# Attention by blocks, groups C and D: ScalarE copies the queries under the shift rows, GpSimd makes their low parts

## The reference

```python
def attend(q, k, v, bias, mask, sink=None):
    s = jnp.einsum('bqhgd,bkhd->bhgqk', qg, k).astype(F32) * (d ** -0.5)
    s = s.reshape(b, hq, tq, -1) + bias
    s = jnp.where(mask, s, NEG_INF)
    ...  # softmax over the keys (and the sink, in C), then the values

def dsa_attend(q, qi, wi, qpos, k, v, ki, kpos, topk, t5_d):
    ...  # sel: the topk keys of each query by the indexer's score
    s = jnp.einsum('bqhd,bqjd->bhqj', q, ks).astype(F32) * (q.shape[-1] ** -0.5) + bias
    s = jnp.where(valid[:, None], s, NEG_INF)
    p = jax.nn.softmax(s, axis=-1).astype(vs.dtype)
    o = jnp.einsum('bhqj,bqjd->bqhd', p, vs)
```

## Time and profile before

| | before |
|---|---|
| median of 3 runs | 4170.81 us (4169.08 to 4173.33) |
| the profiled execution | 4172.25 us, span 4170.4 us |
| mean granted TensorE clock | 0.955 |
| TensorE matmuls (PE) busy | 3779.2 us, 91% of the span |
| TensorE weight loads (PEld) busy | 2628.8 us, 63% |
| VectorE (DVE) busy | 2094.3 us, 50% |
| ScalarE (ACT) busy | 1609.7 us, 39% |
| GpSimd (POOL) busy | 689.1 us, 17% |

### The profile page before, as it was taken

One profiled execution on the slowest core, in us unless ns is written; L12 is line 12 of the kernel. 1 busy time (PEld: TensorE's weight loads), 2 busy tenths in 40 slices (PEclk: granted clock), 3 DMA queues, 4 the chain that ended last, 5 costly groups with the idle time before them and its releaser, 6 DMA issues. The chain is left out here.

```text
span 4170.4 us, 51477 instructions
## 1 busy us (share of the span) xinstructions
PE 3779.2 (91%) x18129; PEld 2628.8 (63%) x18129; DVE 2094.3 (50%) x4989; ACT 1609.7 (39%) x2441; POOL 689.1 (17%) x408
## 2 busy tenths in 40 slices
PE   4899999996999999997999788999868599999798
PEld 3689988995776666665874544444345355555476
DVE  3211111117887344343320199999868766665432
ACT  5111000113454444433320189996445243333332
POOL 4100000002222111111430000000032542211143
PEclk9999999997999999998999899999979699999899
DMA  5222212215455333213431211111242311100243
GB/s 182 66 74 79 67 65 77 68 57 116 98 117 112 72 68 75 65 32 109 163 123 66 63 29 61 61 42 55 97 110 77 89 47 25 37 11 3 107 161 126
DMA packets 222512, 328.50 MB, mean 79 GB/s; under 512 B 22225, under 2 KB 129033, under 8 KB 220897
## 3 DMA queue, kind: packets, MB, share of 16 engines
q1 hardware_dynamic: 173280, 236.21, 19.8%
q10 hardware_dynamic: 43776, 72.50, 4.7%
q0 software_dynamic: 5216, 16.70, 1.9%
HBM read 214.35 MB, written 110.99 MB: 78 GB/s over the span
## 5 line engine op out<-in xcount | busy, mean ns | idle before, releaser
L1028 PE MATMUL attAB_p_o<-attAB_pt,attAB_v 128*65 128x512 f32 (+3 forms) x1120 | 432.8, 484 | 0.2 <-ACT attAB_pt L1075 0.2
L1115 DVE TENSOR_REDUCE attAB_mx<-attAB_p_s 128x1 f32<-128x512 f32 (+2 forms) x360 | 209.5, 609 | 305.7 <-PE attAB_p_s L963 195.0
L508 DVE COPY ab_stage<-ab_pA 128x256 f32<-128x256 f32 (+1 forms) x108 | 56.5, 523 | 602.9 <-PE ab_pA L477 572.3
L2394 DVE TENSOR_SCALAR_CACHE_REDUCE cd_junk<-score,cd_thr 128x512 bf16<-128x512 f32 (+8 forms) x288 | 350.4, 1275 | 1.3 <-DVE cd_thr L2411 0.2
L2432 ACT ACTIVATE cd_gate<-score,cd_thr 128x384 bf16<-128x384 f32 (+2 forms) x192 | 322.3, 1679 | 23.8 <-DVE cd_thr L2411 16.6
L506 ACT ACTIVATE ab_stage<-ab_pA 128x256 f32<-128x256 f32 (+1 forms) x108 | 50.0, 463 | 699.8 <-PE ab_pA L477 679.5
L475 PE MATMUL ab_pA<-ab_W_hi,h_hi 128*128 128x256 f32 x1088 | 309.1, 284 | 3.2 <-PE ab_pA L477 3.1
L1005 PE MATMUL attAB_p_t<-attAB_q_a,attAB_k_a 128*128 128x512 f32 (+3 forms) x560 | 300.2, 540 | 12.7 <-DVE attAB_s_t L1160 11.3
L476 PE MATMUL ab_pA<-ab_W_lo,h_hi 128*128 128x256 f32 x1088 | 307.9, 283 | 0.0
L477 PE MATMUL ab_pA<-ab_W_hi,h_lo 128*128 128x256 f32 x1088 | 307.9, 283 | 0.0
L1637 PE MATMUL attD_p_o<-attD_pt,attD_v 128*65 128x512 f32 x548 | 282.6, 597 | 0.0
(11 more groups left out here) (352 smaller groups left out, 8556.0 us busy)
## 6 DMA issues: line engine op xcount, KB each, us to landing
attAB_raw<-t_k SPq DMA_DIRECT2D x32, 640.0 KB, 7.3
attAB_raw<-t_q SPq DMA_DIRECT2D x32, 640.0 KB, 9.6
t_qg<-cd_stage SPq DMA_DIRECT2D x74, 256.0 KB, 2.0
ab_W_raw<-in_w_ab SPq DMA_DIRECT2D x17, 1024.0 KB, 5.8
mix_o<-t_o SPq DMA_DIRECT2D x34, 512.0 KB, 4.3
t_q<-ab_stage ACTq DMA_DIRECT2D x40, 256.0 KB, 2.0
t_k<-ab_stage ACTq DMA_DIRECT2D x40, 256.0 KB, 2.0
norm_x<-in_x ACTq DMA_DIRECT2D x17, 512.0 KB, 3.7
```

The lines of the kernel that those rows point to most:

```text
L1028: done = nc.tensor.matmul(p_o[u % 2][0:VW, i0 * P:(i0 + n) * P], left, pt[c % NPT][:, at * P:(at + n) * P], start=(c == plan.chunks_of[u][ ...
L2394: nc.vector.tensor_scalar(junk[nth % 2][:, 0:widths[n]], sc[n][:], T[:, n:n + 1], None, ALU.is_ge, ALU.add, accum_out=cnt[s % 2][:, n:n + ...
```

## The change

Four edits, in both stages:

- ScalarE rounds the queries without a factor (L1691, now L1700), and directly behind it makes `q_b` itself, from `q_raw`, with `only_q` as a factor by partition (new, L1701); this counts `q_copied`.
- GpSimd's `prepare` no longer writes `q_b`. In its place it makes the low part in `q_a`, rows 64 to 127, as a subtraction of 64x1024 (L1488), and counts `q_split`. Before it, it waits for its own last instructions of the other kinds, and after it for its own count.
- VectorE's `split_queries` is gone, in the opening and in the loop, and `split_at` with it.
- The factor 1/8 goes into `project_cd`: the evacuations of the query units carry it (L2596), the others a factor of 1.0.

SP's reload of a raw buffer and TensorE's first fill of a block now wait for `q_copied` as well as for `q_split`. The lines behind the edits move: in the changed kernel L1706 is L1716, L1713 is L1723, L1723 is L1733, L1729 is L1739, L1764 is L1774, L1800 is L1804, L1490 is L1496 and L1501 is L1507.

```diff
@@ query_loads
             if b >= NRAW:
                 sp.wait_ge(q_split, b - NRAW + 1)
+                sp.wait_ge(q_copied, b - NRAW + 1)
@@ gpsimd
+                own = {}
+
                 def prepare(b):
                     s = b % NQ
                     pool.wait_ge(q_rounded, b + 1)
-                    nc.gpsimd.tensor_scalar(q_b[s][:], q_a[s][0:AUX].bitcast(F32), only_q[:, 0:1], None, ALU.mult
-                                            ).then_inc(q_copied, 1)
+                    if kind == "D" and b:
+                        pool.wait_ge(near_q, b)
+                    for last, n in own.items():
+                        pool.wait_ge(last, n)
+                    nc.gpsimd.tensor_tensor(q_a[s][HD:P], q_raw[b % NRAW][HD:P], q_a[s][HD:P].bitcast(F32), ALU.subtract
+                                            ).then_inc(q_split, 1)
+                    pool.wait_ge(q_split, b + 1)
@@ add_near and subtract_sinks
                     done.then_inc(near_k, 1)
+                    own[near_k] = b + 1
...
+                    own[sink_less] = u + 1
@@ fill
                         pe.wait_ge(q_split, b + 1)
+                        pe.wait_ge(q_copied, b + 1)
@@ round_queries
-                    nc.scalar.activation(q_a[b % NQ][:], q_raw[b % NRAW][:], ACT.Copy, scale=HD ** -0.5).then_inc(q_rounded, 1)
+                    nc.scalar.activation(q_a[b % NQ][:], q_raw[b % NRAW][:], ACT.Copy).then_inc(q_rounded, 1)
+                    nc.scalar.activation(q_b[b % NQ][:], q_raw[b % NRAW][0:AUX], ACT.Copy, scale=only_q[:, 0:1]).then_inc(q_copied, 1)
@@ vector
-                def split_queries(b):
-                    s = b % NQ
-                    dve.wait_ge(q_copied, b + 1)
-                    nc.vector.scalar_tensor_tensor(q_a[s][HD:P], q_raw[b % NRAW][HD:P], HD ** -0.5, q_a[s][HD:P].bitcast(F32),
-                                                   ALU.mult, ALU.subtract).then_inc(q_split, 1)
...
-                for b in plan.early_blocks:
-                    split_queries(b)
...
-                    for b in plan.split_at[c]:
-                        split_queries(b)
@@ project_cd
-                    nc.scalar.activation(stage[u % 2][:, 0:w], pA[u % BANKS][:, 0:w], ACT.Copy).then_inc(ev[u % BANKS], 1)
+                    scale = HD ** -0.5 if u < 2 * TUNITS else 1.0
+                    nc.scalar.activation(stage[u % 2][:, 0:w], pA[u % BANKS][:, 0:w], ACT.Copy, scale=scale
+                                         ).then_inc(ev[u % BANKS], 1)
```

More of the change, by code:

```diff
@@ L1272, in __init__ @@
         self.blocks_at = [[] for _ in range(NT)]
-        self.split_at = [[] for _ in range(NT)]
         self.near_at = [[] for _ in range(NT)]
@@ L1300, in __init__ @@
                     self.blocks_at[ready].append(p)
-                    self.split_at[max(min(ready + 2, first_fill[u] - 1), ready)].append(p)
                     self.near_at[due[u]].append(p)
```

## The result

The changed kernel takes 4150.70 us, the median of 5 runs (4148.13 to 4152.39); before it was 4170.81. The ratio is 0.995, with a 95% interval of 0.9936 to 0.9965: 20.1 us less. The profiled execution has a span of 4150.6 us, against 4170.4. The forecast was 4157.5, the range 4145 to 4173.

A forecast was written before the change was run, and what follows sets the result against it. The prediction took VectorE to set C's loop, with TensorE 0.72 us a block behind, and TensorE to set D's. C +3.65 and D -16.9 gave -13.3: 4172.25 to 4158.95, median 1.44 lower, 4157.5 us; range 4145 to 4173.

The forecast's parts named there:

- The projection: Projection ahead of C and D: evacuations get an immediate factor instead of 1; taken as zero, 4.3 us of ScalarE at worst.
- C's opening: Start of C: block 2's query path shorter, -1.8; TensorE's wait of 1.25 goes but ScalarE's extra pass stands there, -0.2.
- C's loop: 26 units of C: VectorE's removed pass gives -6.95, ScalarE's new pass costs 1.05 in 12 blocks, +12.6; sum +5.65.
- D's first wait: D's opening, TensorE's 10.97 wait for the first shift: VectorE splits cached keys from 3264.0 to 3266.3, ending earlier, -4.6.
- rival A: D's opening: port changes hands at each GpSimd boundary, cached-key split ends at 3262.1, another 4.2 us gained, 4153.3; chance 0.12.
- The second wait: D's opening, TensorE's 9.36 wait for block 2's queries: fills come at 3285.05 instead of 3291.99, -6.95.
- The third wait: D's opening, fourth block: shift is ready before TensorE comes, -3.56; the clock's fall behind the wait goes too, -1.8.
- D's loop: Loop of D: VectorE's 1.2 us and ScalarE's extra 1.05 a block are hidden beside TensorE, 0.
- Rival C: Loop of D: ScalarE's pass makes TensorE wait, 1.15 in each of the last 15 blocks, +17.3, 4174.8; chance 0.14.
- Rival B: Loop of C: ScalarE's pass costs nothing because TensorE has slack that busy time hides, -12.6, 4144.9; chance 0.10.
- rival D: D's opening: GpSimd's work stays one queue, cached-key split comes last, TensorE's 3.56 wait stays; D gives 9.4, 4165.0; chance 0.14.

The follow-up runs named there:

- the kernel with it and the form alone: Kernel before, with factor 1/8 in the projection and VectorE's low-part pass as plain subtraction; GpSimd still writes q_b: 4170.72 us, ratio 1.0001.
- the gap: Changed kernel with ScalarE's q_b pass two chunks later for blocks 4 and up, between an exponent and the next shift rows: 4137.83 us, ratio 0.9917.
- the keep: Changed kernel with ScalarE's q_b pass one chunk later for blocks 4 and up, behind `keep` and ahead of the unit's second exponent: 4144.20 us.
- the doubled pass: Changed kernel with ScalarE's 66x1024 pass done twice a block, the second into a spare tile, in both stages: 4190.27 us, one run.
- GpSimd keeps both: Changed kernel with the pass over q_b back on GpSimd, ahead of its subtraction: 4173.10 us.
- GpSimd keeps its pass, VectorE doesn't wait for it: Kernel before with factor in projection and plain VectorE subtraction, GpSimd's q_b pass reading raw queries, VectorE waiting for ScalarE's copy alone: 4159.70 us.

## Why the prediction was right, and where it was not

The sign, the places and which of them gains or loses were right; the size was 13.3 where the median moved by 20.1, and 4150.7 lies below the forecast's own range of 4152 to 4164. By its steps:

- **The projection**, zero: 576 and 577 ns, and the kernel with it and the form alone has a ratio of 1.0001.
- **C's opening**, -1.8 and -0.2. The first fill of block 2 came at 3073.16 against 3075.70, 2.54 earlier, of which 0.77 are keys and a start that came earlier (the shift rows ahead of it at 3066.67 against 3067.44): 1.77 for 1.8. Behind it another 1.78 went (-4.32 in all at the second turn), where the prediction had let ScalarE's first pass take up nearly all of it. That pass fell into the first unit of the loop instead.
- **C's loop**, -6.95 + 12.6 = +5.65: measured +6.93. Thirteen passes lie in the 26 units, not twelve; 13 x 1.05 = 13.65, and -6.95 + 13.65 = +6.7. The unit lengths of 4.18 and 5.2 came as written (4.17 and 5.25). Together with the opening and the end, C cost 2.03 where the forecast had 3.65. That the pass is paid because of its place was only argued then; the gap, the keep and the doubled pass show it.
- **D's first wait**, -4.6. This is the step that failed. The split of the cached keys got in at the end of the near tile, as rival A had it at a chance of 0.12, and ended at 3264.20. The first shift rows came at 3265.62 for 3272.35, and C had ended 2.03 later: 8.76 gained in C's frame, where rival A's price was 8.8. The two first waits together gave 15.70 for 4.6 + 6.95 = 11.55. The prediction took the pattern from VectorE's passes of before, with the same near tiles in GpSimd's queue; but ahead of those near tiles stood GpSimd's pass over q_b, which the change takes away. That the earlier entry comes from this is not shown (last section).
- **The second wait**, -6.95. The fill of block 2 came 13.69 earlier, 15.72 in C's frame, and the first shift rows, ahead of it, 8.76 (above): 6.96 is left for this one.
- **The third wait**, -3.56 - 1.8 = -5.36: measured 5.38, between the turns around it. The clock's share is not separated from the wait's.
- **D's loop**, 0: 0.6 us remain there, less than runs differ. Rival C (ScalarE's pass stalls D) fell with the doubled pass: 1.8 us of D's stage for twice the work.
- **Rival B** (the pass costs nothing in C) fell with the waits of 0.91 for the exponent, **rival D** (GpSimd bounds D's opening) with the first wait at 3.92 and the third gone.

With -8.8 in place of -4.6 the working gives -17.5; the 1.6 in C and the 0.6 of D's loop make it -19.7, against 19.65 at D's last turn.

What the prediction didn't see is which part of the change earns. Taken one after the other, from the medians: factor and form 0 (4170.72), the pass over q_b from GpSimd to ScalarE -20.7 (4150.02), the low part from VectorE to GpSimd +0.7, less than the runs' spread (4150.70), and ScalarE's pass into the gap -12.9 (4137.83). The third is worth something only after the fourth: without it, 4141.67.

## What to carry to other kernels

Work that is moved to an engine with idle time is paid by where it stands in that engine's queue: list the instructions behind it and ask which of them another engine waits for; a pass of 1.04 us cost 1.06, 0.56 or 0.08 a block at three places, and a longer queue on GpSimd cost C through a sink difference of 0.2 us. Undo a change that has several parts one part at a time; here the part that its diff is mostly about was worth nothing until a second edit was made. And take a pattern of contention over to new code only with everything that stood in the queues around it.

## What the hardware showed that was not expected

**Who gets in between GpSimd's instructions.** VectorE's passes with two tiles in SBUF wait where they ask while GpSimd runs a near tile, in the thirteen kernels in which one does. What differs is for how long. In the ten kernels whose GpSimd has no TENSOR_SCALAR pass, one such wait in D's opening met a queue with more near tiles behind the running one, and each ended with the running instruction (0.5 to 3.5 us). In the kernel before and in the two that keep that pass and VectorE's low part, the ten low-part passes that met such a queue each passed over at least one boundary (14.77 for two, 6.69, 8.90 and 6.83 us). The Trainium skill ("SBUF — State Buffer", "Who interferes with whom") says that whoever issues first holds the shared port pair for its whole instruction, and that a VectorE instruction with two SBUF inputs contends with a GpSimd instruction that reads SBUF. By that rule VectorE comes in at the next boundary: the ten kernels agree, the other three don't. Nor did the split of the cached keys wait for a TENSOR_SCALAR, which reads SBUF too: it asked 1.12 us into one and took its own 2.28 (GpSimd keeps both). The low-part pass at 3269.40 (GpSimd keeps its pass, VectorE doesn't wait for it) did wait, though it asked 0.39 us into one. The split's rows:

```profile
3273.07 2.84 POOL L1484 TENSOR_SCALAR attD_q_b<-attD_q_a,attD_only_q 66x1024 fp32r<-66x1024 f32 x1
3275.99 2.69 POOL L1491 TENSOR_TENSOR attD_q_a<-attD_q_raw,attD_q_a 64x1024 fp32r<-64x1024 f32 x1
```

```profile
3274.19 2.28 DVE L1776 TENSOR_TENSOR attD_c_b<-attD_raw,attD_c_a 64x2048 fp32r<-64x2048 f32 x1 [12.69 <-ACT attD_c_a L1697]
```

VectorE's form is ruled out as the cause. Why a TENSOR_SCALAR among GpSimd's instructions makes a low-part pass wait on stays open: no run here changed that alone.

**The clock after short waits.** A wait of TensorE of 0.91 us in each block (the changed kernel) and of about 1.55 (GpSimd keeps both) left the granted clock at 1.00 from 3087 to 3203. Behind the last wait of 1.55 it fell, to 0.72 over 3216 to 3222, and the two matmuls of 1.04 us took 1.94:

```profile
3216.28 1.94 PE L1649 MATMUL attC_p_o<-attC_pt,attC_v 128*65 128x512 f32 x2 [1.55 <-ACT attC_pt L1735]
```

With 1.97 a block (the pass twice) it held for four blocks and fell in each of the nine behind them, to 0.76 over 7 us, and such a block lost some 1.5 us more. So a stall's price has a step in it that its length doesn't tell: waits of 1.55 and 1.97 us each stand on both sides of it.
